# Splitting the weights of a two-layer encoder 1024 columns at a time instead of 512

## The reference

```python
u, gate_a, u3, gate_b, c_q, c_kv, k_r, gate_c, merge, ... = split(x @ w_in)
y_a = glu(gelu(s5_scan(u)))              # state-space scan, both directions
y_b = hyena(short_conv3(u3), filters)    # long convolution, order 2
y_c = attention(rms(c_q) @ w_uq, rms(c_kv) @ w_ukv)
mix = sum(sigmoid(merge[b]) * ((silu(gate[b]) * y[b]) @ w_lift[b]) for b in "abc")
ple = (gelu(x @ w_g) * p) @ w_ple
x   = layer_norm(alpha * x + mix @ w_out + ple)
```

## Time and profile before

| | before |
|---|---|
| median of three runs | 2877.02 us (2876.92 to 2879.37) |
| the profiled execution | 2877.76 us |
| its span, first to last instruction | 2876.2 us |
| PE busy | 2709.4 us, 94% |
| DVE busy | 1876.5 us, 65% |
| ACT busy | 1297.3 us, 45% |
| mean granted clock of TensorE | 0.980 |
| DMA | 411.19 MB, mean 143 GB/s |
| chain of work that ended last | 87% of it on PE |

### The profile page before, as it was taken

The page is one execution under the profiler, slowest core; times in us unless marked ns, Lnnn a source line. Parts: engine busy times, 40 slices in busy tenths (PEclk is TensorE's granted clock), DMA queues, the critical chain, the costliest instruction groups (busy, mean ns, idle before and its releaser), DMA issues.

```text
span 2876.2 us, 50752 instructions
## 1 busy us (share of the span) xinstructions
PE 2709.4 (94%) x18088; PEld 2429.8 (84%) x18088; DVE 1876.5 (65%) x3312; ACT 1297.3 (45%) x2319; POOL 108.7 (4%) x202
## 2 busy tenths in 40 slices
PE   5899999989999999999869999998999999999996
PEld 5799999877987879999858999987789878799996
DVE  6878787634567766565487878786255677565655
ACT  4555555624543233453334555556255433244532
POOL 1100000000000000000021000000000000000000
PEclk9999999999999999999989999999999999999999
DMA  6444444333452334555354444442344423245552
GB/s 224 151 144 149 149 143 149 124 125 133 147 169 96 111 103 137 182 176 171 115 170 151 149 145 149 149 144 101 133 152 142 162 96 118 88 158 182 176 169 88
DMA packets 115096, 411.19 MB, mean 143 GB/s; under 512 B 15300, under 2 KB 15322, under 8 KB 114448
## 3 DMA queue, kind: packets, MB, share of 16 engines
q1 hardware_dynamic: 106704, 390.12, 40.4%
q0 software_dynamic: 8256, 19.26, 2.1%
HBM read 403.02 MB, written 6.29 MB: 142 GB/s over the span
## 4 chain that ended last, share of the span: by engine, by line
PE 87%; DVE 6%; issue 3%; ACT 2%; DMA 1%; DVEq 0%; PEldq 0%; POOLq 0%; POOL 0%; ACTq 0%; PEld 0%; SPq 0%
PE bank L1447 36%; PE bank L1475 18%; PE bank L1477 9%; PE bank L1429 5%; PE bank L1568 2%; PE bank L1545 2%; PE bank L1759 2%; PE bank L1527 2%; PE bank L1723 2%; PE bank L1746 1%; PE bank L1512 1%; PE bank L1562 1%; PE bank L1636 1%; DVE WL L380 1%; PE bank L1661 1%
## 5 line engine op out<-in xcount | busy, mean ns | idle before, releaser
L366 ACT ACTIVATE WH<-ring 128x512 fp32r<-128x512 f32 x1360 | 855.7, 631 | 1278.7 <-PE bank L1447 725.0
L380 DVE TENSOR_TENSOR WL<-ring,WH 128x512 fp32r<-128x512 f32 x848 | 574.7, 690 | 533.9 <-ACT WH L366 528.7
L1475 PE MATMUL bank<-XX,WH 128*128 128x512 f32 x2304 | 826.1, 402 | 69.3 <-DVE XX L520 46.5
L1447 PE MATMUL bank<-XX,WH 128*128 128x256 f32 x3712 | 683.3, 286 | 12.6 <-DVE WL L380 8.2
L1477 PE MATMUL bank<-XX,WL 128*128 128x256 f32 x2304 | 646.6, 281 | 0.0
L1447 PEld LDWEIGHTS bank<-XX,WH 128*128 128x128 f32 x3712 | 581.0, 192 | 30.7 <-issue 23.9
L1475 PEld LDWEIGHTS bank<-XX,WH 128*128 128x128 f32 x2304 | 438.0, 190 | 171.8 <-DVE XX L520 46.9
L1447 PE MATMUL bank<-XX,WL 128*128 128x256 f32 x1856 | 526.3, 284 | 0.0
L371 DVE TENSOR_TENSOR WL<-ring,WH 128x512 fp32r<-128x512 f32 x512 | 350.9, 688 | 141.0 <-ACT WH L366 136.9
L1477 PEld LDWEIGHTS bank<-XX,WL 128*128 128x128 f32 x2304 | 439.8, 191 | 0.0
L1447 PEld LDWEIGHTS bank<-XX,WL 128*128 128x128 f32 x1856 | 357.2, 192 | 0.0
(11 more groups left out here) (297 smaller groups left out, 3649.3 us busy)
## 6 DMA issues: line engine op xcount, KB each, us to landing
ring<-in_blocks SPq DMA_DIRECT2D x736, 512.0 KB, 3.3
ARENA<-in_bc POOLq DMA_DIRECT2D x2, 2048.0 KB, 8.4
ARENA<-in_decay POOLq DMA_DIRECT2D x8, 512.0 KB, 4.6
ARENA<-in_x SPq DMA_DIRECT2D x1, 2048.0 KB, 9.8
u_scratch<-ARENA POOLq DMA_DIRECT2D x16, 128.0 KB, 2.2
ARENA<-u_scratch POOLq DMA_DIRECT2D x64, 32.0 KB, 2.8
y_scratch<-ARENA POOLq DMA_DIRECT2D x16, 128.0 KB, 2.0
ARENA<-y_scratch POOLq DMA_DIRECT2D x64, 32.0 KB, 2.7
```

Of the source, the lines that this page charges most:

```text
L366: nc.scalar.activation(wh[q], raw(which[0], q), ACT.Copy).then_inc(wh_ready[q], 1)
L380: vec.tensor_tensor(wl[q], raw(which[0], q), wh[q].bitcast(F32), ALU.subtract).then_inc(w_used[slot(which[0], half)], 1)
L1447: ins = mm(o, w_, x_, start=start and i == 0 and n == 0, stop=stop and i == 7 and n == 2)
L1475: ins = mm(bank[b][:, :], h, xx[:, :, k, :], start=(k == 0), stop=(k == DT - 1), skip_group_check=True)
```

## The change

Outside S5 a half of a block is split by one instruction of each engine. ACT waits for both `parts_used` of the half, copies 128 x 1024 and counts a new semaphore, `wh_half[half]`. DVE waits for that, subtracts 128 x 1024 and counts `w_used` up by two. S5 keeps its quarters under new names, `make_wh_quarters` and a `make_wl_quarter` with its own count. PE's program and SP's stay as they are.

```diff
+        wh_half = [sem(f"wh_half{i}") for i in range(2)]
         def make_wh(act, half, layer, *which):
             act.wait_ge(w_loaded[slot(which[0], half)], load_number(layer, *which) * 16)
             for q in (2 * half, 2 * half + 1):
+                act.wait_ge(parts_used[q], split_number(layer, *which))
+            nc.scalar.activation(WH[:, half * HALF:(half + 1) * HALF], slots[slot(which[0], half)], ACT.Copy).then_inc(wh_half[half], 1)
+
+        def make_wh_quarters(act, half, layer, ct, j):
+
+            which = (B_S5 + j + 1, ct, 8)
+            act.wait_ge(w_loaded[slot(which[0], half)], load_number(layer, *which) * 16)
+            for q in (2 * half, 2 * half + 1):
 
                 act.wait_ge(parts_used[q], split_number(layer, *which))
                 nc.scalar.activation(wh[q], raw(which[0], q), ACT.Copy).then_inc(wh_ready[q], 1)
...
         def make_wl(eng, vec, layer, *which, halves=(0, 1)):
 
             for half in halves:
-                for q in (2 * half, 2 * half + 1):
-
-                    eng.wait_ge(wh_ready[q], split_number(layer, *which))
-                    vec.tensor_tensor(wl[q], raw(which[0], q), wh[q].bitcast(F32),
-                                      ALU.subtract).then_inc(w_used[slot(which[0], half)], 1)
+                cols = slice(half * HALF, (half + 1) * HALF)
+                eng.wait_ge(wh_half[half], half_number(layer, *which))
+                vec.tensor_tensor(WL[:, cols], slots[slot(which[0], half)], WH[:, cols].bitcast(F32),
+                                  ALU.subtract).then_inc(w_used[slot(which[0], half)], 2)
...
-                            make_wh(act, half, layer, B_S5 + j + 1, ct, 8)
+                            make_wh_quarters(act, half, layer, ct, j)
```

More of the change, by code:

```diff
@@ L341, in split_number, with half_number @@
             return layer * SPLITS + (block_ - skipped + 1) + turn * per
+        def half_number(layer, block_, turn=0, per=0):
+            skipped = 0 if block_ <= B_S5 else 8 * WT if block_ <= B_LIFT0 else 8 * WT + (UNSPLIT[0] if block_ < B_W3 else UNSPLIT[1] if block_ <= B_OUT0 else UNSPLIT[2])
+            return layer * (SPLITS - 8 * WT) + (block_ - skipped + 1) + turn * per
         def hyc(o, step, n=0, b=4):
@@ L365, in make_wh, with quarter_number, make_wl_quarter @@
                 act.wait_ge(parts_used[q], split_number(layer, *which))
+            nc.scalar.activation(WH[:, half * HALF:(half + 1) * HALF], slots[slot(which[0], half)], ACT.Copy).then_inc(wh_half[half], 1)
+        def quarter_number(layer, ct, j):
+            return layer * (8 * WT) + (ct * 8 + (j + 1))
+        def make_wh_quarters(act, half, layer, ct, j):
[3 more added lines that the diff above has]
+                act.wait_ge(parts_used[q], split_number(layer, *which))
                 nc.scalar.activation(wh[q], raw(which[0], q), ACT.Copy).then_inc(wh_ready[q], 1)
-        def make_wl_quarter(q, layer, *which):
-            nc.vector.wait_ge(wh_ready[q], split_number(layer, *which))
+        def make_wl_quarter(q, layer, ct, j):
+            which = (B_S5 + j + 1, ct, 8)
+            nc.vector.wait_ge(wh_ready[q], quarter_number(layer, ct, j))
             nc.vector.tensor_tensor(wl[q], raw(which[0], q), wh[q].bitcast(F32),
@@ L651, in add_block @@
                         free(v.tensor_tensor(tile_, tile_, bank[j % 2][:, 0:T], ALU.add), j % 2)
-                    wl_for = lambda j, q: make_wl_quarter(q, layer, B_S5 + j + 1, ct, 8)
+                    wl_for = lambda j, q: make_wl_quarter(q, layer, ct, j)
                     def coeff(at, n):
@@ L1210, in _ @@
                     turned(1)
-                    make_wh(act, 0, layer, B_S5 + 3, ct, 8)
+                    make_wh_quarters(act, 0, layer, ct, 2)
                     act.wait_ge(frac_ready, layer * WT + (ct + 1))
@@ L1217, in _ @@
                     st.wait()
-                    make_wh(act, 1, layer, B_S5 + 3, ct, 8)
+                    make_wh_quarters(act, 1, layer, ct, 2)
                     a.activation(cos_, cos_, ACT.Sin, bias=half_pi, scale=-2 * PI_LOW)
@@ L1242, in _ @@
                             if t == 1:
-                                make_wh(act, d, layer, B_S5 + 7, ct, 8)
+                                make_wh_quarters(act, d, layer, ct, 6)
                         free(ins, 4 + d)
```

## The result

The changed kernel takes 2969.26 us (median of 4 runs, 2966.55 to 2973.03), before 2878.19 in the same session: ratio 1.0316, 95% interval 1.0298 to 1.0334, so 91 us slower. The forecast was 2930 with a range of 2905 to 2957. Direction right, size too small by 39 us.

The account below looks back on a forecast made before the run. It took PE, busy 94% of the span, as the bound. `ax` 13.7, `hyc` 22.9, ple 7.6 and 3.4 for gate waits and collisions gave 47.6; with 5 for the clock, 52.6 on 2877.76: about 2930 us, range 2905 to 2957.

Parts of the forecast that it names:

- the tenth block: Hyena stage: PE's gap ahead of 943.11 was to grow from 2.36 to about 3.3 us, the product starting 0.94 later.
- The later `w_used`: Ring loads: `w_used` comes 0.95 us later for a slot, wanted again 11.4 us later; DMA cost put at nothing.
- Wrong step 1: Lift, out, most of ple, `lifta`, MLA: chain of 2.77 us fits PE's 2.86 per half and costs nothing.
- The first rival: New chain fits nowhere; handovers together 0.2 us longer make 296 halves late, 30 us more, 2960; chance 10%.
- my 1.5: Stray collisions: small work between splits makes a half late by some tenths where the chain fits; 1.5 us in all.
- 7, 5 and 5: Lower bounds: `ax` counted at half (-7), half of `hyc`'s just-in-time places free (-5), no clock loss (-5).
- 9 and 10 more: Upper bounds: all eight clock losses (+9) and a third of the thin margins missed (+10).
- Wrong step 2: Hyena stage (`hyc`): later product, just-in-time work, smaller places and stage end, 11.4 us per layer, together +22.9.
- (b): Hyena stage: ACT's longer copy and DVE's subtraction start the product at the tenth block 0.94 us later, all PE idle time.
- Wrong step 3: Clock: some eight gaps grow to 2.5 to 3.5 us; about three bring a half-clock stretch, 1.7 us each: +5.
- `ax` 13.7: `ax`: DVE's serial steps start later behind longer splits; +6.5 less 0.1 in layer 0, +7.3 in layer 1.
- ple 7.6 and 1.9: ple: MIXH, MIXL and two half-width DVE passes delay halves, 3.8 per layer; the first gate result's wait, 0.95 per layer.

Follow-up runs that it names:

- e_stream: Kernel before the change, with halves on ACT and DVE only in MLA, lift and out, quarters elsewhere: 2900.69 us, ratio 1.0067.
- e_wait: Kernel before with all copies and subtractions kept; outside S5 ACT waits for both parts of a half before its first copy: 2910.22 us, ratio 1.0097.
- e_act: Kernel before with ACT copying halves outside S5 while DVE still subtracts quarters: 2938.58 us, ratio 1.0198.
- e_dve: Kernel before with DVE subtracting halves outside S5 while ACT still copies quarters: 2919.08 us, ratio 1.0138.
- the four groups: Kernel before with halves only in MLA, lift and out; only in `ax`; only in Hyena; only in ple: +20, +18, +43, +17 us.
- v_behind: Kernel before, quarters everywhere, some Hyena-stage DVE work moved ahead of the split of the next block's half 0: 2866.51 us, ratio 0.9951.
- e_link: e_stream, but a first half that announces no result frees its last quarter with its own last matmul: 2894.13 us, ratio 1.0047.

## Why the prediction was right and wrong

**Right.** PE is the bound, the two engines' busy time buys nothing, and the change is a loss because a split's first usable part comes later. The prediction had busy time on DVE fall by 68 us; it fell by 56. It multiplied mean durations, which counts the overlap of neighbours twice; the busy time in its own row, 574.7, less 518.0 is 57. At the tenth block the gap was to be about 3.3 and is 3.46. The later `w_used` is indeed hidden but for 1.2 us: PE waits twice for a load of the ring, 0.6 us each, where it did not before, and ACT's two waits for one are shorter (3.5 us in all, 5.9 before). As for the direction, the Trainium skill, "Perfetto Trace Analysis", section "Optimizing Scalar/DVE Operations", says that breaking instructions up may let work complete sooner where Scalar and Vector aren't saturated but cause bubbles elsewhere; the runs agree, 91 us slower for merging at 61% and 41% busy.

**Wrong step 1: "the new chain fits, by 0.09 us, and costs nothing."** It costs 19 us in MLA, lift and out by the matched matmuls, 20 by e_stream. The terms that were mis-sized are the handovers: 0.47 instead of 0.32 from matmul to copy, 0.10 instead of 0.03 from copy to subtraction. The first was taken from an old copy, which waits for one part only, behind a matmul for which PE had not waited: the wait for both parts makes it 0.40 (e_wait, e_act), the slower matmul of a half that PE has waited for makes it 0.47. The second was taken from a subtraction of 512 columns, and the new one has 1024. So the chain is 2.93 us without a stall and 3.00 with one, and a late half frees the other buffer late and so makes the next half late as well. The rule to have seen: a link belongs to the instruction that it was measured on, with its waits and its size, and to whether its engine stood waiting. My row for the stalled case, 0.50 at 35.37, would not have given it either: its matmul has 512 columns, and behind such a one the old copy starts after 0.43 us where PE has not waited (the middle of 193). The first rival had the condition, handovers together 0.2 longer (0.23 was measured), and its sign, a period of 2.9 us or more in lift and out (3.00 in the rows of lift above), is there. Its 30 us were nearer than my 1.5, and 2957 as the upper end left it out. That end does not follow from my terms either: 2930 less 7, 5 and 5 is 2913, and with 9 and 10 more it is 2949, not 2908 and 2952.

**Wrong step 2: the Hyena stage, 22.9 us, measured 41.7.** Three terms. (a) Four places per layer were missed, at the first matmul of a plain half (before, 851.70, 879.70, 983.24, 1011.24): there DVE is behind with its own work when the copy is long done, PE starts as soon as one quarter is subtracted, and now needs both: +0.96 to +1.03 each, 4.0 per layer. In e_act and e_dve each of these costs 0.55 to 0.58. They cost nothing before, so no list of waits had them; I had looked only at work that PE waits for behind a split, not at splits that PE waits for behind work. (b) Each serial place lost 1.1, not 0.94: 0.07 by the later start of the long subtraction and 0.08 by the later start of a copy that waits for both parts. (c) The clock, 10 us ungranted per layer instead of 5.

**Wrong step 3: the clock, "about three gaps", +5.** In the Hyena stage alone, stretches behind the gaps of 3.46 us at L1777 and around L1704 had half the clock where before they had the full one, 1.7 us each, about 5 us per layer; `ax` has more of them (the first matmul behind the stall, at 36.69, takes 0.77 us). Summed, about 15 us: the mean clocks, 0.9799 over 2876 us and 0.9754 over 2971 us, leave 58 and 73 us ungranted. This is an upper bound, since a part of that is time in which PE waited anyway.

**`ax` 13.7, measured 18.9; ple 7.6 and 1.9, measured 15.3.** The places were right and each step was too short: DVE's steps behind the third block start at 49.99 where I had 48.2, `add_input` behind them at 53.50 where I had 51.7, and the copies at 84.50 where I had 81.9. What is missing is the handovers and the low clock: behind the stall at 36.69 the matmul takes 0.77 us and the copy starts 0.89 later, not 0.50. Another 0.7 us in layer 0 need not be the change's: DVE's first steps of `ax` wait for a DMA and start at 29.76 instead of 29.05, and over all the kernels here, with quarters or halves, that start lies anywhere from 28.66 to 29.76. In ple the gap ahead of the block behind MIXH grew by 1.48 and that behind MIXL by 1.59 (forecast 1.4 and 1.5), and a wait for the first result by 1.9 (forecast 0.95), as two matmul groups there both stall; the rest is small stalls of the kind of step 1.

Left open: why the sum of the four groups is some 6 us above the whole; it is within the intervals. And what decides which gap brings the low clock: no run was made for the clock alone.

## What to carry to other kernels

Where a consumer begins on the first part of a buffer, the grain of the producers is latency: price a coarser grain by when the first usable part is there and by what cover the early part had, not by the engines' busy time. When a chain is to fit a period, take each link from an instruction with the waits and the size of the new one, and from a row in which the consumer stood waiting; here three missing terms of 0.07 to 0.08 us turned a chain that fits by 3% into one that misses at every turn. And where DVE holds both a split and work that PE stands idle for, the order of the two is worth more than the size of either: moving the work ahead was worth 14 us, with no instruction saved.

## What the runs showed of the hardware

- Behind a stall, the first matmul of 256 columns takes 0.36 us instead of 0.28, in the kernel before as in the changed one.
- A copy on ACT that waits for one part starts 0.04 us after the end of the matmul that frees it, one that waits for both parts 0.10 to 0.12, with 512 columns (e_wait) as with 1024 (e_act). From the matmul's start that is 0.32 and 0.40 us, and 0.47 behind a stall.
- DVE's subtraction of 1024 columns starts 0.10 us after the end of the copy that it waits for, one of 512 columns 0.03 to 0.04, whichever size the copy has. In the rows of e_dve above a copy of 512 from 1152.73 ends at 1153.36 and the subtraction starts at 1153.46.
- A gap of 1.18 us and those of 2.36 us at the product of the tenth block left the granted clock at 1.00 in v_behind and in the kernel before, the gap of 3.46 at the same place brought 0.50 for 3 us and more. The length alone doesn't decide. In `ax` a gap of 2.31 was followed by 0.50 before, and in e_link, with quarters, this same place had a gap of 2.24 and then the stretch below, granted 0.57. Over the kernels here, four such places in each, the clock fell within 1.5 us of the end of 11 of 12 gaps of 3.46 to 3.48 us, and of 3 of 20 gaps of 2.24 to 2.39.

```profile
943.00:946.00 3.00, 3.00 (x9) 2.34 (x9) 1.61 (x5) 0.90 (x2) 0.00 (x0) 0.57 0.00 0
```
